# Row gathers of a mixture-of-experts combine, issued from the experts' block instead of the next stage

## The reference, cut to what matters

```python
for l in range(DEPTH):                       # DEPTH = 2
    h = rms_norm(x, norm_mix_g[l])
    proj = h @ w_in[l]
    ...
    h = rms_norm(x, norm_ffn_g[l])
    x = x + hierarchical_moe(h, ...)         # for each token: gate1 * y[expert1] + gate2 * y[expert2]
return x
```

## Time and profile before

| | us |
|---|---|
| median of 3 runs | 2136.66 |
| lowest, highest | 2130.24, 2138.98 |
| profiled execution, span from first to last instruction | 2143.1 |
| TensorE busy in it | 2031.7 |
| VectorE, ScalarE, GpSimd busy in it | 669.1, 375.5, 61.0 |

### The profile page before, as it was taken

How to read it: one execution, slowest core, us unless ns; L and a number is a source line. 1 busy time by engine, 2 the same in 40 slices (tenths; PEclk the granted TensorE clock), 3 DMA queues, 4 the chain that set the end, 5 groups by cost and what they waited for, 6 DMA issues and landing times. The chain is left out here.

```text
span 2143.1 us, 27989 instructions
## 1 busy us (share of the span) xinstructions
PE 2031.7 (95%) x11762; PEld 1101.5 (51%) x11762; DVE 669.1 (31%) x1343; ACT 375.5 (18%) x729; POOL 61.0 (3%) x127
## 2 busy tenths in 40 slices
PE   8999998899899999999799999989989999999996
PEld 6446985545544444443254488654555444444442
DVE  4245464423331111111043556551443111111112
ACT  3221222413200000000022222150330000000001
POOL 3001000000000000000010010000000000000001
PEclk9999798999999999999999999999999999999998
DMA  8000002200489999999860000022026999999997
GB/s 334 1 1 1 2 3 97 109 37 1 162 340 428 428 427 429 427 428 429 354 264 0 0 2 2 9 118 118 0 118 243 421 427 428 428 429 428 428 427 265
DMA packets 51550, 481.91 MB, mean 225 GB/s; under 512 B 7216, under 2 KB 12080, under 8 KB 23792
## 3 DMA queue, kind: packets, MB, share of 16 engines
q1 hardware_dynamic: 49136, 471.91, 52.7%
q0 software_dynamic: 2304, 8.39, 1.1%
HBM read 461.14 MB, written 19.14 MB: 224 GB/s over the span
## 5 line engine op out<-in xcount | busy, mean ns | idle before, releaser
L2004 PE MATMUL bank<-ring,hT 128*64 128x512 f32 x2080 | 471.2, 595 | 12.1 <-DMA ring<-in_we 8.9
L2004 PEld LDWEIGHTS bank<-ring,hT 128*64 128x64 f32 x2080 | 143.5, 137 | 285.0 <-issue 265.7
L862 PE MATMUL bank<-hT,ring 128*128 128x512 f32 (+1 forms) x608 | 263.3, 593 | 1.8 <-DVE hT L312 1.0
L1997 PE MATMUL bank<-arena 128*128 128x256 f32 x1088 | 252.9, 386 | 0.0
L2011 PE MATMUL bank<-ring,arena 128*64 128x512 f32 x1040 | 237.5, 598 | 9.7 <-DMA ring<-in_we 7.4
L1997 PEld LDWEIGHTS bank<-arena 128*128 128x128 f32 x1088 | 202.6, 191 | 73.9 <-issue 48.7
L862 PEld LDWEIGHTS bank<-hT,ring 128*128 128x128 f32 (+1 forms) x608 | 114.0, 189 | 148.2 <-issue 147.2
L2176 DVE COPY hT<-bank 128x512 f32<-128x512 f32 x68 | 47.0, 691 | 405.7 <-PE bank L1997 405.6
L2011 PEld LDWEIGHTS bank<-ring,arena 128*64 128x64 f32 x1040 | 69.1, 136 | 145.0 <-issue 132.6
L2156 ACT ACTIVATE arena<-bank 128x256 f32<-128x256 f32 x65 | 25.0, 384 | 672.5 <-PE bank L1983 672.5
L1697 PE MATMUL bank<-hT,ring 128*128 128x512 f32 x256 | 110.3, 593 | 2.9 <-PEq L96 2.9
(11 more groups left out here) (430 smaller groups left out, 2069.0 us busy)
## 6 DMA issues: line engine op xcount, KB each, us to landing
ring<-in_we SPq DMA_DIRECT2D x195, 2048.0 KB, 17.6
expert_rows<-arena SPq DMA_DIRECT2D x130, 128.0 KB, 15.0
ring<-in_w_in SPq DMA_DIRECT2D x6, 2048.0 KB, 20.0
ring<-in_w_out SPq DMA_DIRECT2D x4, 2048.0 KB, 10.3
ring<-in_wm SPq DMA_DIRECT2D x2, 2048.0 KB, 17.0
ring<-in_w_in SPq DMA_DIRECT2D x2, 1920.0 KB, 17.3
ring<-in_w_in SPq DMA_DIRECT2D x2, 1664.0 KB, 27.7
ring<-in_w_in SPq DMA_DIRECT2D x2, 1152.0 KB, 30.1
```

The costliest lines, as they stand in the source:

```text
L862: last = nc.tensor.matmul(B[n % 4][0:w, :], ins_units[unit][:, k, u0:u0 + w], hT[:, k, :], start=k == 0, stop=k == KD - 1)
L1997: last = nc.tensor.matmul(bank[:, o:o + GS], htok[:, i, k * P:(k + 1) * P], selg[z][:, i, :], start=i == 0, stop=i == NT - 1)
L2004: last = nc.tensor.matmul(bank[CAP * j:CAP * j + CAP, :], x[:, k, :], up_w(u, j, k), start=k == 0, stop=k == KD - 1)
```

## The change

The gathers leave the two combine stages. They are issued by POOL in the experts' block, after a wait for the row numbers (`s_sl`, new) and one for every stored row (`s_yo`, the wait that SP has as well). They no longer write `arena`, in which the experts' block still has its token rows, but units 2 and 4 of the ring. The next layer's `w_in` for these units (2, 4 and 5; unit 5's home begins inside ring unit 4) then waits for all four flips. The overflow experts take units 0, 1, 5. The keep-busy matmuls ahead of the flips go from 10 to 5, and 6 are put at the end of TensorE's list in the experts' block.

```diff
-        yg = [[arena[:, 2048 * i + 1024 * k:2048 * i + 1024 * k + 1024] for i in range(NT)] for k in range(2)]
+        yg = [[ring[:, (2, 4)[k], 1024 * i:1024 * i + 1024] for i in range(NT)] for k in range(2)]
...
                         eng.wait_ge(s_yg1[NT - 1], 16 * layer)
-                        load_w_in(eng, lay, (1, 0, 2, 4, 5))
+                        load_w_in(eng, lay, (1, 0))
+                        eng.wait_ge(s_cf, NT)
+                        load_w_in(eng, lay, (2, 4, 5))
...
-                    if layer:
-                        combine_gather(eng, ys_d[0:NE * CAP, :])
...
-                        keep_busy(B[7], 10, 4 * P)
+                        keep_busy(B[7], 5, 4 * P)
...
-            MORE_SLOTS = (2, 4, 5)
+            MORE_SLOTS = (0, 1, 5)
...
             with nc.Block() as block:
+                @block.gpsimd
+                def _(eng):
+                    eng.wait_ge(s_sl, 1)
+                    for z in range(2):
+                        eng.wait_ge(s_yo[z], 32 * (NE // 2 + (2 if FINAL and z == 0 else 1)))
+                    combine_gather(eng, ys_d if FINAL else ys_d[0:NE * CAP, :])
...
                     if FINAL:
                         turn(GROUPS, 0, 0, False, False)
+                    keep_busy(B[7], 6, 4 * P)
...
+                    eng.sem_inc(s_sl, 1)
                     gather_out(GE + 1, 1, 0)
...
-            @block.gpsimd
-            def _(eng):
-                combine_gather(eng, ys_d)
...
-                keep_busy(B[7], 10, 4 * P)
+                keep_busy(B[7], 5, 4 * P)
```

More of the change, by code:

```diff
@@ L1863, in build @@
             s_sg, s_hd, s_dn, s_ys = sem("silu_done"), sem("hidden_ready"), sem("down_done"), sem("rows_ready")
-            s_ml = sem("overflow_list")
+            s_ml, s_sl = sem("overflow_list"), sem("row_numbers_ready")
             s_yo = [sem(f"rows_written{u}") for u in range(2)]
```

## The result

| | kernel before | changed kernel |
|---|---|---|
| median, us | 2137.82 (20 runs) | 2154.03 (20 runs) |
| lowest, highest | 2126.99, 2161.33 | 2147.74, 2171.47 |
| ratio, 95% interval | | 1.0084 (1.0064 to 1.0104) |

The changed kernel is slower by 0.84%: of 2137.8 us that is 18 us, 13.7 to 22.2 (the medians differ by 16.2). The forecast was plus 11.3.

A forecast was written before the change was run, and what follows sets the result against it. The prediction took the stage to wait for its slowest arrival, then the first add for TensorE's keep-busy matmuls. Plus 4.9 us at layer 1 and 6.4 at the end, 11.3 on 2136.7, gave 2148 us, range 2138 to 2155.

The forecast's parts named there:

- Gathers moved: Hand-over from experts to combine: all eight gathers issue before POOL's barrier, so both openings come 10.6 us later.
- rival 2: End of the experts' block: POOL's barrier waits for the gathers' landings, each opening up to 5.6 us later, 2159 us; chance 0.04.
- POOL started: Experts' block: POOL's first gather starts 0.4 us after the last stores land, taken between near 0 and 0.8.
- The train: POOL's eight gather issues, one at a time, take 10.2 us at layer 1 and 10.3 at the end.
- The first adds: Combine: VectorE's first add starts 7.1 us after the opening at layer 1 and 8.4 at the end.
- the first add waits for TensorE's keep-busy matmuls: Combine: tile 0's flip stands behind ten keep-busy records, 6.2 us at layer 1 and 7.4 at the end.
- Nothing for the loads: Next layer's w_in: units 2, 4, 5 and the parameters leave later but stay hidden, at no cost.
- Nothing for the six keep-busy matmuls: TensorE's end of the experts' block: 12 records, 5.2 us, beside SP's wait and POOL's train, cost nothing.
- Rival 1: Experts' block: the barrier lets the stage through while POOL still issues, minus 5.1 us, 2131.6 us; chance 0.10.
- Rival 3: Combine: TensorE's clock rises early at both places, ending the keep-busy bound: plus 6.4, 2143 us; inside the forecast's 0.84.
- The sum of 11.3: Both places together: plus 4.9 us at layer 1 and plus 6.4 us at the end.

The follow-up runs named there:

- the explicit wait: Changed kernel, plus POOL waiting for all 16 landing semaphores of the gathers before its experts' block ends: 2162.4 us in one run.
- the filler memsets: Changed kernel, plus five or ten memsets on POOL between the eighth gather and the end of its block: 2161.1 and 2162.4 us, one run each.
- the two early gathers: Changed kernel with only tile 0's gathers in the experts' block, the other six at the next stage's start: median 2149.8 us, ratio 1.0064 to the kernel before.
- the end-only kernel: Changed kernel with layer 0's gathers back in the next stage, only the last combine's issued early: median 2150.2 us, ratio 1.0043 to the kernel before.
- the late wait: Kernel before, with the wait for the last stores moved from SP's block end to POOL in the next stage: 2131.6 and 2134.3 us, ratios 0.9975 and 0.9973.
- the two by-changes: Kernel before, with w_in units 2, 4, 5 waiting for the flips and 5 keep-busy matmuls instead of 10: median 2144.5 us, ratio 1.0022.

## Why the prediction was wrong

**The step that failed** is "Gathers moved", where the opening was put at 1064.1 + 0.4 + 10.2 + 2.4. It let the barriers begin when POOL had issued its eighth gather. They begin when the gathers have landed; the explicit wait and the filler memsets fit that, and the two early gathers leave no other theory of the three. The opening is 8.1 and 7.5 us behind the end of the eighth gather instead of 2.4 and 2.0: 5.7 and 5.5 us more. This was rival 2, with 5.6 at each place, 2159 us and a chance of 0.04. The argument against it did not bear on it: that POOL issues the next gather without waiting for the last one's landing says nothing of what its end of block waits for. No row of the kernel before could tell. Gathers are the last thing POOL does only in its last block, and there POOL is through at 2129.6, while the other engines work on to the end at 2143.1.

**The other terms** were right or off by little. POOL started 0.9 us after the landing, for which I took 0.4. The train was 9.9 and 9.7 us for 10.2 and 10.3: none was stretched, and none ran beside VectorE's pairs. The first adds came 6.9 and 6.9 us after the opening for 7.1 and 8.4. With the landing put in, the forecast's sum would have been 22.5, and the path shows 21.1. The reading that the first add waits for TensorE's keep-busy matmuls was right: it waited 1.1 and 3.3 us for the flip.

**Nothing for the loads** was right: the projection waits only for `hT`. **Nothing for the six keep-busy matmuls** was right with POOL's wait as cover: they end at 1068.7, 1.7 us behind the stores' landing and 17 ahead of the opening. What was said of them without that cover was wrong: they would "end about 0.9 us ahead of the opening and still cost nothing", and the end-only kernel shows a barrier held by them and 1.5 us lost.

**Rival 1** fell: the barrier let nothing through. **Rival 3**, an early rise of the clock, did not come: the ten records took 6.0 us at both places, not 4.3, with 0.50 granted in their first 2 us.

**Its form.** The sum of 11.3 stood on the edge of half a per cent, so the forecast gave nearly equal chances to slower and within; slower was right, by more than the sum. That the median of 2154.0 us still lies within 2138 to 2155 is no merit of the mechanism: the forecast's own terms ended at 2153, and the rest is the widening for the spread of the runs.

## What to carry to other kernels

Before moving a DMA in front of a barrier, ask what the barrier waits for on the issuing engine. Here it waited for the landing of GpSimd's gathers and not of SyncE's stores, so in this kernel the gathers belong behind the barrier, where their flight overlaps the first consumers, and a wait for stores may go there too. Keep-busy matmuls have a price as soon as the wait that hid them is gone. Leaving them out has one too, so read the granted clock in the stretch that follows.

## What the runs showed of the hardware

GpSimd's end of block waited until its indirect DMAs had landed: the opening followed the last landing by 2.4 and 1.8 us with two gathers and by 2.6 and 2.1 with eight. SyncE's did not wait for its stores: in the late wait the opening came 2.7 and 2.2 us after the last store's issue. With two in flight a gather landed in 4.7 us (median of each place), with eight in 6.1 and 6.4.

TensorE's clock can fall in the sparse work between flips. It did so with ten keep-busy matmuls ahead of them (late wait, after a pause of 1.5 us) and with five, and did not at layer 1 of the kernel before. The Trainium skill says that pauses between bursts can bring it down ("TensorE: Matmul & The Clock Gate", section "HAM oscillation — how this bites in real kernels"); the trace of the two by-changes agrees, with 0.50 granted from 1062 to 1064 after pauses of 2.7 and 2.3 us between five keep-busy matmuls and two flips.
